# First layer: late modulation sums split in high and low words on GpSimd before their sum over partitions, and the last three sums of a chunk in steps 5, 6 and 7 instead of 7, 8 and 9

## What is computed

```python
def _modulation(cond, w_mod, b_mod):
    m = jax.nn.silu(cond) @ w_mod + b_mod
    return jnp.split(m, 3, axis=-1)

for l in range(DEPTH):
    sh, sc, g = _modulation(c, w_mod[l], b_mod[l])
    shc, scc, gc = _modulation(c_ctx, w_mod[l], b_mod[l])
    h = x * (1.0 + sc) + sh
    q, k, v, z = jnp.split(h @ w_in[l], 4, axis=-1)
    ...
    out = (y * jax.nn.silu(z)) @ w_out[l]
    x_new = _layer_norm(DEEPNORM_ALPHA * x + (1.0 + g) * out, ln_g[l], ln_b[l])
```

## Time and profile before

| | |
|---|---|
| median of 3 runs | 1840.8 us (1840.79 to 1842.08) |
| profiled execution, first to last instruction | 1840.5 us |
| PE busy | 1804.3 us, 98% |
| DVE busy | 1264.2 us, 69% |
| ACT busy | 925.7 us, 50% |
| POOL busy | 268.9 us, 15% |

### The profile page before, as it was taken

The page is one execution under the profiler, slowest core; times in us unless marked ns, Lnnn a source line. Parts: engine busy times, 40 slices in busy tenths (PEclk is TensorE's granted clock), DMA queues, the critical chain, the costliest instruction groups (busy, mean ns, idle before and its releaser), DMA issues. The chain is left out here.

```text
span 1840.5 us, 31074 instructions
## 1 busy us (share of the span) xinstructions
PE 1804.3 (98%) x10621; PEld 1556.4 (85%) x10621; DVE 1264.2 (69%) x2317; ACT 925.7 (50%) x1680; POOL 268.9 (15%) x219
## 2 busy tenths in 40 slices
PE   7999999999999999999999999999999999999998
PEld 4888988898988888878878889888888888898886
DVE  6677777767676767756868475765848484757658
ACT  2555555555555555550146455454646364554500
POOL 3100000000000000356331010101000010102951
PEclk9999999999999999999999999999999999999999
DMA  9312121212121212326420010100010100101343
GB/s 344 89 48 82 49 85 45 83 49 82 40 81 53 75 59 62 98 70 200 146 81 24 18 40 11 46 11 34 11 46 11 34 23 23 34 11 45 99 143 126
DMA packets 73663, 124.92 MB, mean 68 GB/s; under 512 B 41312, under 2 KB 41472, under 8 KB 73488
## 3 DMA queue, kind: packets, MB, share of 16 engines
q1 hardware_dynamic: 68496, 106.48, 18.1%
q0 software_dynamic: 2384, 8.39, 1.7%
q10 hardware_dynamic: 2736, 9.44, 1.3%
HBM read 106.54 MB, written 17.73 MB: 68 GB/s over the span
## 5 line engine op out<-in xcount | busy, mean ns | idle before, releaser
L524 PE MATMUL acc<-h_hi,w_hi 128*128 128x512 f32 (+1 forms) x1408 | 524.8, 373 | 3.1 <-DVE h_lo L449 1.6
L524 PE MATMUL acc<-h_hi,w_lo 128*128 128x512 f32 (+1 forms) x1408 | 508.6, 361 | 0.0
L524 PE MATMUL acc<-h_lo,w_hi 128*128 128x512 f32 (+1 forms) x1408 | 507.8, 361 | 0.0
L524 PEld LDWEIGHTS acc<-h_hi,w_lo 128*128 128x128 f32 x1408 | 265.3, 188 | 41.5
L524 PEld LDWEIGHTS acc<-h_hi,w_hi 128*128 128x128 f32 x1408 | 265.8, 189 | 40.1 <-DVE h_lo L449 4.7
L524 PEld LDWEIGHTS acc<-h_lo,w_hi 128*128 128x128 f32 x1408 | 266.3, 189 | 33.7
L1651 DVE TENSOR_REDUCE stats<-acc 128x1 f32<-128x1280 f32 x128 | 189.6, 1487 | 43.9 <-PE acc L1750 43.2
L1561 ACT ACTIVATE far_prob<-acc,stats 128x1280 f32<-128x1280 f32 x128 | 170.1, 1329 | 28.3 <-DVE stats L1651 26.6
L1568 ACT ACTIVATE far_pt<-acc 128x512 f32<-128x512 f32 (+1 forms) x192 | 101.0, 526 | 163.0 <-PE acc L1759 159.7
L1750 PE MATMUL acc<-k_dup,q_stack 128*128 128x512 f32 (+1 forms) x768 | 177.1, 367 | 1.8 <-ACT far_prob L1561 0.3
L1162 ACT ACTIVATE near_pt_hi<-acc 128x384 fp32r<-128x384 f32 (+1 forms) x208 | 110.4, 531 | 124.0 <-PE acc L1349 105.8
(11 more groups left out here) (210 smaller groups left out, 2906.4 us busy)
## 6 DMA issues: line engine op xcount, KB each, us to landing
w_raw<-in_w_in SPq DMA_DIRECT2D x64, 512.0 KB, 3.4
near_late_slots<-in_w_mod SPq DMA_DIRECT2D x64, 256.0 KB, 2.7
w_raw<-in_w_out SPq DMA_DIRECT2D x16, 512.0 KB, 3.3
w_raw<-y_t POOLq DMA_DIRECT2D x14, 448.0 KB, 5.2
y_t<-y SPq DMA_DIRECT2D x7, 640.0 KB, 3.1
modulation_rows<-in_w_scale SPq DMA_DIRECT2D x8, 512.0 KB, 6.4
modulation_rows<-in_w_mod SPq DMA_DIRECT2D x8, 512.0 KB, 6.4
out_rows<-in_x SPq DMA_DIRECT2D x8, 512.0 KB, 5.1
```

Of the source, the lines that this page charges most:

```text
L524: mm = nc.tensor.matmul(m.bank(self.bank_of(j, c), w), wt[:, b % 2, k, :], ht[:, k, t0:t0 + w], start=(k == 0 and i == 0), stop=(k == KT - ...
```

## The change

- `late_slots` and `late_acc` are allocated in a scope that is closed at once, so that two new tiles of the same sizes, `late_high` and `late_low` (fp32r, a rounded 32-bit type), take their place in SBUF.
- New on POOL, once for each of the first seven chunks: `split`. After the chunk's last sum it casts both accumulators to the high words, and subtracts these from the accumulators to make the low words.
- `reduce` waits for the split and sums high and low words by four fp32r matmuls instead of two fp32 ones. `pick` is fp32r, and is written by four small `tensor_scalar` instructions instead of four `memset`s.
- Sums 5, 6 and 7 stand at the ends of steps 5, 6 and 7.
- `load` of u = 7 stands in SP's list ahead of the second and third group of bias patches. The loads of the next chunk's u = 0 and 1 wait for `reduced`, since their slots now hold the high words.

```diff
-        self.late_slots = sb("late_slots", [P, 2, 512])
-        self.late_acc = sb("late_acc", [P, 2, 512])
+        with ExitStack() as sums:
+            self.late_slots, self.late_acc = (sums.enter_context(nc.sbuf_tensor("near_" + n, [P, 2, 512], F32))
+                                              for n in ("late_slots", "late_acc"))
+        self.late_high, self.late_low = sb("late_high", [P, 2, 512], F32R), sb("late_low", [P, 2, 512], F32R)
...
-            nc.vector.memset(m.pick[:, r, r:r + 1], 1.0)
-            nc.vector.memset(m.pick[:, r, 1 - r:2 - r], 0.0)
+            nc.vector.tensor_scalar(m.pick[:, r, r:r + 1], m.cond[:, 0, 0:1], 0.0, 1.0, ALU.mult, ALU.add)
+            nc.vector.tensor_scalar(m.pick[:, r, 1 - r:2 - r], m.cond[:, 0, 0:1], 0.0, None, ALU.mult)
...
     def load(self, sp, c, u):
-        if u >= 2:
+        if u >= KT:
+            sp.wait_ge(self.reduced, CREDIT + c * 1 + 1)
+        elif u >= 2:
             sp.wait_ge(self.summed, CREDIT + c * 2 * KT + 2 * (u - 1))
...
+    def split(self, pool, c):
+
+        pool.wait_ge(self.summed, CREDIT + c * 2 * KT + 2 * KT)
+        for cnd in range(2):
+            self.nc.gpsimd.tensor_copy(self.high[cnd], self.acc[cnd]).then_inc(self.high_done, 1)
+        for cnd in range(2):
+            pool.wait_ge(self.high_done, c * 2 + cnd + 1)
+            self.nc.gpsimd.tensor_tensor(self.low[cnd], self.acc[cnd], f(self.high[cnd]), ALU.subtract).then_inc(self.split_done, 1)
+
     def reduce(self, pe, c, bank):
 
-        pe.wait_ge(self.summed, CREDIT + c * 2 * KT + 2 * KT)
+        pe.wait_ge(self.split_done, c * 2 + 2)
         for cnd in range(2):
-            mm = self.nc.tensor.matmul(self.m.psum[0:2, bank, :], self.m.pick[:, cnd, :], self.acc[cnd],
-                                       start=(cnd == 0), stop=(cnd == 1))
+            for part in (self.high, self.low):
+                mm = self.nc.tensor.matmul(self.m.psum[0:2, bank, :], self.m.pick[:, cnd, :], part[cnd],
+                                           start=(cnd == 0 and part is self.high), stop=(cnd == 1 and part is self.low))
...
+                        late.load(sp, c, KT - 1)
                         for kind in (1, 2):
...
-                        for u in (7, KT, KT + 1):
+                        for u in (KT, KT + 1):
...
+                for c in range(NCH - 1):
+                    late.split(pool, c)
...
-                        if NU - 3 <= step < NU and not last:
-                            late.sum(v, c, step - NU + 3 + 5)
+                        if NU - 5 <= step < NU - 2 and not last:
+                            late.sum(v, c, step - NU + 5 + 5)
```

More of the change, by code:

```diff
@@ L107, in __init__ @@
         self.stats = sb("stats", [P, 96])
-        self.pick = sb("pick", [P, 2, 2])
+        self.pick = sb("pick", [P, 2, 2], F32R)
         self.psum = stack.enter_context(nc.psum_tensor("acc", [P, 8, 512], F32))
@@ L354, in __init__ @@
         self.summed, self.reduced, self.row_ready, self.row_stored = sem("summed"), sem("reduced"), sem("row"), sem("stored")
+        self.high_done, self.split_done = sem("high"), sem("split")
+        self.high = [near.late_high[:, i, :] for i in range(2)]
+        self.low = [near.late_low[:, i, :] for i in range(2)]
         self.counters = self.loaded + [self.summed, self.reduced, self.row_ready, self.row_stored]
     def load(self, sp, c, u):
-        if u >= 2:
+        if u >= KT:
+            sp.wait_ge(self.reduced, CREDIT + c * 1 + 1)
+        elif u >= 2:
             sp.wait_ge(self.summed, CREDIT + c * 2 * KT + 2 * (u - 1))
@@ L393, in reduce_last @@
         for cnd in range(2):
-            mm = self.nc.tensor.matmul(self.m.psum[0:2, bank, :], self.m.pick[:, cnd, :], self.acc[cnd],
+            mm = self.nc.tensor.matmul(self.m.psum[0:2, bank, :], f(self.m.pick[:, cnd, :]), self.acc[cnd],
                                        start=False, stop=(cnd == 1))
```

## The result

The changed kernel takes 1848.8 us (median; 1847.7 to 1849.0), against 1840.8 us before. The ratio is 1.0038, with a 95% interval of 1.0025 to 1.005: slower by 0.4%. The profiled execution spans 1847.1 us, 6.6 us more than the earlier trace rows. The times of either kernel lie in two groups some 1.2 us apart, and the median before is of the lower group and the median after of the upper, so that like with like the change costs 6.9 to 7.0 us and not 8.0.

The account below looks back on a forecast made before the run. PE, busy 1804.3 of 1840.5 us, was taken as the bound. 7 x (1.32 - 0.23) = +7.6 us gave 1848.1, plus 0.3 from profiled span to median: 1848.4 us, 0.4% slower, range 1843.5 to 1852.5.

Parts of the forecast that it names:

- Sum 6: End of step 6: delays unit 7's row maximum, then through ACT and DVE PE's `values` in step 7; +1.32 us a chunk.
- Sum 5: End of step 5: DVE's waits there cover it; taken as 0, at most +0.1 us a chunk.
- The reduction: Step 10: four fp32r matmuls take 0.96 us instead of 1.81, but `values` waits for DVE; -0.23 us a chunk.
- The 0.09 us ahead of the reduction: Step 10: PE's wait for the chunk's last sum, expected to go if the split is done.
- The split: POOL's casts and subtractions, up to 5.2 us a chunk, hidden with over 4 us to spare; cost 0.
- The price of 0.11 us: DVE's product of two SBUF tiles takes 0.53 us instead of 0.42 when POOL works; taken as 0 here.
- SP and the start: Later loads and bias patches cost 0; four small DVE instructions at the start, 0.7 us once if nothing covered them.
- A: Step 7: the late row maximum is absorbed and only the reduction's term is left; 1839.2 us, chance 0.07.
- B: As A, and `values` in step 10 starts as soon as the reduction is over; 1834.2 us, chance 0.06.
- C: Step 10: fp32r with two weight columns is as slow as before, no gain; 1850.0 us, chance 0.08.
- D: Step 7: the new wait lowers PE's clock, 1.5 us a fall, 10.5 in seven chunks; 1858.9 us, chance 0.05.

Follow-up runs that it names:

- the second run: Kernel before with sums 5, 6 and 7 at the ends of steps 5, 6 and 7 and the early load, no split, fp32 reduction: 1850.1 us, ratio 1.0051.
- the run with 16 columns: Kernel before with the fp32 reduction cut to the first 16 of 512 columns: 1838.7 us, ratio 0.9987.
- the third run: Changed kernel with the sums back at the ends of steps 7, 8 and 9, split and fp32r reduction kept: 1868.1 us, ratio 1.0146.
- the fill: Changed kernel with sums at 5, 7 and 8, and the next chunk's last product piece moved behind `turn` of unit 9: 1834.6 us, ratio 0.9963.
- the first run: Changed kernel with sums 5, 6 and 7 at the ends of steps 5, 7 and 8: 1838.7 us, ratio 0.9988.

## Why the prediction was right

**The bound and the place.** PE's list was the right thing to read: PE's busy time fell and the time rose by what PE waits. The absence of an idle mark before the row at 233.76 in the earlier trace rows, with the scores ready just before, told that step 7 had no slack.

**Sum 6, +1.32 us a chunk.** Measured +1.34 in step 7, +1.29 a chunk in the run with the sums alone, and (1848.8 - 1838.7) / 7 = 1.44 from the changed kernel to the run at 5, 7 and 8; the last holds some 1 us of another origin (last section), and from trace to trace, where the last looped chunk ends at 732.12 and 722.89, it is 9.2 / 7 = 1.32. All of the links through ACT are in the rows above. That the cause is the place and nothing else is shown from three sides: putting sum 6 one step later takes the loss away, moving sum 7 does not, and moving a sum to the end of step 4 makes it again in step 5.

One reading of the prediction was off without an effect: three transposes hold PE for about 0.25 us and not 0.33 (in step 7 before, from 234.09 to `values` at 234.34), so the wait that was already there was 0.25 us and not 0.17.

**Sum 5, 0.** Right: the waits of L1378 for L1268 are 5.1 us in total with and without it, and in step 6 of the second chunk 0.34 and 0.33.

**The reduction, -0.23 us a chunk.** Too small by 0.09: it is 0.32 in step 10. The 0.15 us from DVE's end to PE's start was taken from step 7; here it is 0.06 (DVE ends at 253.63 + 0.69 = 254.32, PE starts at 254.38), and that is the whole error. Three more readings were off and don't enter the term. The 0.09 us ahead of the reduction was no wait for the last sum, as the second run showed. The four transposes hold PE for 0.35 us and not 0.43, and the four fp32r matmuls for 1.02 and not 0.96; these nearly cancel, 1.37 against 1.39. None of this changes that the chain through ACT and DVE holds `values`: the run with 16 columns shows it.

**The split, 0.** Right, with more room than thought: 3.7 us and not up to 5.2, as a cast takes 0.62 us and not 1.29. DVE's rows beside it have their old lengths (L1268 0.56 and 0.69, L1263 0.41). Without cover it costs `values` 2.76 us a chunk and not 5.2, as the third run showed. The price of 0.11 us for a product of two SBUF tiles beside POOL's work was too small. In the changed kernel no product meets the split, but in the runs with sums at 5, 7 and 8 (with and without the fill) and at 5, 6 and 8 the one of step 9 does, in all seven looped chunks, and it takes 1.10 to 1.12 us instead of 0.42, 0.7 more. The first run, second chunk:

```profile
246.69 2.54 POOL L392 TENSOR_TENSOR near_late_low<-near_late_acc,near_late_high 128x512 fp32r<-128x512 f32 x2
248.41 1.10 DVE L1281 TENSOR_TENSOR y<-y,gate 128x256 f32<-128x256 f32 x1
250.97 0.69 DVE L1268 TENSOR_TENSOR near_pt_lo<-acc,near_pt_hi 128x512 fp32r<-128x512 f32 x1 [1.36 <-ACT near_pt_hi L1182]
```

It costs no time there, since DVE waits another 1.36 us before the next row that PE needs. Ahead of a row like the one of step 7 it might cost time; no run has it there.

**SP and the start, 0.** Right: the run at 5, 7 and 8 has the early load and the later patches and no loss. The patches end at 246.41 instead of 244.40. PE's first row of L1378 starts at 111.44, against 111.49 before, so the four new instructions at the start cost nothing.

**The rivals.** A and B fall with step 7's wait; the work that B counted on is a wait, and needs another edit to become a gain. C falls with the 0.23 us of L399. D did not come. Ten us of each looped chunk around the wait of step 7 show a granted clock of 1.00 in the changed kernel; two of the seven stretches:

```profile
236.00:246.00 10.00, 8.65 (x69) 8.13 (x68) 8.45 (x23) 6.67 (x18) 2.92 (x4) 1.00 0.27 53
331.00:341.00 10.00, 8.65 (x68) 8.13 (x68) 8.84 (x22) 6.74 (x18) 2.48 (x4) 1.00 0.26 54
```

The fall came in the run without cover, where the wait is 3.57 us.

**Sum.** 7 x (1.34 - 0.32) = 7.1 us against the predicted 7.6; the end of the last looped chunk (`L1358`, now `L1378`) moved from 725.18 to 732.12, 6.9 us. The medians are 8.0 apart, and about 1 us of that is not the change (last section). So it is in part luck that the predicted 1848.4 is only 0.4 under the median. The median "0.3 above the profiled span" was part of that luck: a time is 1.8 us above its own span (1848.9 beside 1847.1), so the profiled execution before took about 1842.3, and was one of the longer ones. From span to span the forecast was 1848.1 and the measurement 1847.1, 1.0 less. The mechanism and the two terms stand by the rows.

## What to carry to other kernels

- A small instruction on an engine that is idle for a third of the time costs nothing or nearly its full length (1.32 us; measured 1.34 and 1.03), by where it stands. Look for the idle mark behind the place: if the next row has none and what it needs was ready, and the bound engine waits for something further down that list, the insert is paid on the bound engine.
- Before work on the bound engine is shortened, look at what the next instruction waits for. If a chain of others ends at the same time, the gain is a wait until something is moved into it.
- Splitting work off to an idle engine needs as much lead as it takes there. Here a place one step later for the last two sums had lead enough, and missed the tight step. Look also at what the first engine does meanwhile: its products of two SBUF tiles took 0.7 us longer beside the subtraction.

## What the runs showed of the hardware that was not expected

- A matmul with two fp32r weight columns and 512 moving columns follows its like at 0.23 to 0.24 us, as the projection with 128 weight columns does; the first one behind fp32 transposes has a distance of 0.32, and the projection's first one there 0.31 (224.73 to 225.04 in the changed kernel). From four fp32 transposes to an fp32 matmul with two weight columns it is 0.52 to 0.53 us, and to an fp32r one 0.35: 0.17 more, with no wait for DVE. Why it is so was not tested.
- A DVE product of two SBUF tiles (128 x 256, fp32) takes 0.42 us alone, 0.52 or 0.53 beside POOL's work in the last chunk and 1.10 to 1.12 beside POOL's subtraction of two SBUF tiles; the subtraction keeps its 1.29 us. Rows that read PSUM keep their length beside it.
- Whether the clock falls in the last chunk differs from execution to execution. Before, the stretch from 784 to 787 us stood at 0.53; after, it fell at the same place:

```profile
791.00:795.00 4.00, 3.98 (x19) 3.94 (x20) 2.11 (x7) 2.09 (x6) 2.36 (x1) 0.57 0.34 124
```

In the first run, with the same last chunk 2.3 us earlier than before, it stayed up:

```profile
770.00:780.00 10.00, 7.38 (x55) 6.66 (x54) 8.93 (x25) 8.24 (x17) 6.50 (x3) 1.00 0.37 119
780.00:790.00 10.00, 8.92 (x63) 8.21 (x64) 8.76 (x27) 8.53 (x19) 4.05 (x3) 1.00 0.35 118
```

The fall costs about 1.2 us: from one L1358 to the next it is 11.71 us before (784.07 to 795.78), and in the first run, by L1378, 10.54 (781.80 to 792.34). Of the ten profiled executions it fell in four (before, after, the sums alone, the fill behind the short reduction; distance 11.6 to 11.7) and stayed up in six (10.5 to 10.6). For the last three of these four the listed time is 1.0 to 1.5 us above the lowest of the same kernel; in the six it is within 0.4 us of the lowest, but for the run without cover. So it explains the distance of about 1.2 us between times of one kernel (1840.8 and 1842.0 before, 1847.7 and 1848.9 after), as far as the profiled executions show. A difference of about 1 us between two medians of this kernel says nothing; the length of a chunk in the traces says more.
